# Rotary halves swapped by transfers inside SBUF instead of a matrix product, in a two-layer block kernel on one core

## What is computed

```python
def apply_rope(x, cos, sin):
    xf = x.astype(jnp.float32)
    x1, x2 = jnp.split(xf, 2, axis=-1)
    out = jnp.concatenate([x1 * cos - x2 * sin, x2 * cos + x1 * sin], axis=-1)
    return out.astype(x.dtype)
...
    u = jnp.einsum("bsd,de->bse", h, w_in)
    offs = np.cumsum(IN_SPLITS)[:-1].tolist()
    a_b, a_c, a_x, q, k, v, c_in = jnp.split(u, offs, axis=-1)

    y_a = a_b * causal_depthwise_conv(a_c * a_x, short_conv_w)

    q = apply_rope(q.reshape(b, s, 2, N_DIFF_HEADS, DIFF_HEAD_DIM), cos, sin)
    k = apply_rope(k.reshape(b, s, 2, N_DIFF_HEADS, DIFF_HEAD_DIM), cos, sin)
...
    o = diff_attention(q, k, v, lam)
...
    c = c_in + glu_b
    c = c[..., :CONF_WIDTH] * jax.nn.sigmoid(c[..., CONF_WIDTH:])
    c = causal_depthwise_conv(c, conf_dw_w) + conf_dw_b
    y_c = jax.nn.silu(layernorm(c, conf_ln_g, conf_ln_b))
```

## Time and profile before

| | us |
|---|---|
| median of 3 runs (lowest, highest) | 2680.19 (2677.57, 2681.05) |
| the profiled execution's own time | 2680.19 |
| its span in the trace | 2678.9 |
| PE busy | 2562.9 (96%) |
| DVE, ACT, POOL busy | 1103.3, 945.4, 1211.0 |

### The profile page before, as it was taken

One profiled execution on the slowest core, in us unless ns is written; L12 is line 12 of the kernel. 1 busy time (PEld: TensorE's weight loads), 2 busy tenths in 40 slices (PEclk: granted clock), 3 DMA queues, 4 the chain that ended last, 5 costly groups with the idle time before them and its releaser, 6 DMA issues.

```text
span 2678.9 us, 32969 instructions
## 1 busy us (share of the span) xinstructions
PE 2562.9 (96%) x12952; PEld 2112.5 (79%) x12952; DVE 1103.3 (41%) x2303; ACT 945.4 (35%) x1437; POOL 1211.0 (45%) x1597
## 2 busy tenths in 40 slices
PE   6999999999999999998999999999999999999998
PEld 5777888887777888886778788877777787888886
DVE  7965111126964211137656764423345523311112
ACT  4553322234453222244433233324453433322221
POOL 5114665653125656554332332344323554565653
PEclk8999999999999999999999999999998999999998
DMA  4442223225432222232110111122222231223222
GB/s 156 124 111 79 94 81 103 102 83 151 126 95 79 101 92 99 96 108 94 50 48 32 48 37 44 48 95 86 87 79 89 100 110 64 95 92 105 94 89 76
DMA packets 41371, 237.32 MB, mean 89 GB/s; under 512 B 4736, under 2 KB 5888, under 8 KB 18560
## 3 DMA queue, kind: packets, MB, share of 16 engines
q1 hardware_dynamic: 38912, 218.43, 23.4%
q0 software_dynamic: 2304, 16.78, 3.1%
HBM read 214.22 MB, written 4.19 MB: 82 GB/s over the span
## 4 chain that ended last, share of the span: by engine, by line
PE 84%; DVE 10%; ACT 3%; POOL 2%; issue 1%; DMA 0%; SPq 0%; DVEq 0%; ACTq 0%
PE PB L1757 67%; PE PB L1795 4%; PE PB L1759 4%; DVE cc L2413 2%; POOL WL L2788 2%; ACT WH L2016 1%; PE PB L1952 1%; PE PB L1971 1%; PE PB L1769 1%; PE PB L1777 1%; PE PB L1959 1%; PE PB L1919 1%; PE PB L1983 1%; PE PB L1999 1%; PE PB L1940 0%
## 5 line engine op out<-in xcount | busy, mean ns | idle before, releaser
L2788 POOL TENSOR_TENSOR WL<-WR,WH 128x256 fp32r<-128x256 f32 (+1 forms) x1444 | 1041.9, 757 | 789.1 <-ACT WH L2016 789.1
L1757 PE MATMUL PB<-HH,WH 128*128 128x512 f32 x1992 | 803.8, 404 | 12.2 <-ACT HH L2031 10.0
L1757 PE MATMUL PB<-HL,WH 128*128 128x512 f32 x1992 | 783.5, 393 | 1.9 <-DVE HL L2309 1.9
L1757 PE MATMUL PB<-HH,WL 128*128 128x512 f32 x1992 | 520.3, 397 | 2.6 <-POOL WL L2788 2.6
L2016 ACT ACTIVATE WH<-WR 128x2048 fp32r<-128x2048 f32 (+1 forms) x209 | 371.5, 1778 | 260.9 <-PE PB L1757 254.2
L1757 PEld LDWEIGHTS PB<-HH,WH 128*128 128x128 f32 x1992 | 378.4, 190 | 102.8 <-issue 14.3
L1757 PEld LDWEIGHTS PB<-HL,WH 128*128 128x128 f32 x1992 | 378.3, 190 | 80.0 <-issue 3.6
L1757 PEld LDWEIGHTS PB<-HH,WL 128*128 128x128 f32 x1992 | 366.0, 189 | 76.6 <-issue 3.9
L1757 PE MATMUL PB<-BL,WH 128*128 128x512 f32 x848 | 334.1, 394 | 0.8 <-DVE BL L2318 0.8
L1757 PE MATMUL PB<-BH,WH 128*128 128x512 f32 x784 | 310.6, 396 | 2.7 <-ACT BH L2045 2.7
L1757 PE MATMUL PB<-BH,WL 128*128 128x512 f32 x784 | 197.6, 396 | 5.4 <-POOL WL L2788 5.4
(11 more groups left out here) (344 smaller groups left out, 3103.1 us busy)
## 6 DMA issues: line engine op xcount, KB each, us to landing
WR<-in_w_gu SPq DMA_DIRECT2D x66, 1024.0 KB, 4.8
WR<-in_w_dn SPq DMA_DIRECT2D x48, 704.0 KB, 4.1
WR<-in_w_in SPq DMA_DIRECT2D x22, 1024.0 KB, 4.9
WL<-WR POOLq DMA_DIRECT2D x16, 1024.0 KB, 7.0
WR<-in_qkv SPq DMA_DIRECT2D x12, 1024.0 KB, 4.8
WR<-in_w_out SPq DMA_DIRECT2D x8, 1024.0 KB, 4.8
WR<-in_qk SPq DMA_DIRECT2D x8, 1024.0 KB, 4.8
WR<-in_gb SPq DMA_DIRECT2D x4, 1024.0 KB, 4.8
```

The costliest lines, as they stand in the source:

```text
L1757: ins = pe.matmul(out[:, 0:n], wt[:, k * cols + j * P:k * cols + (j + 1) * P], x[:, k, 0:n], start=first, stop=last)
L2788: ins = g.tensor_tensor(m.WL[u % 2][:, part], m.WR[u % 2][:, part], f32(m.WH[u % 2][:, part]), ALU.subtract)
```

## The change

The swap of halves is made by four transfers inside SBUF of 32 partitions each (64 KB), issued by SP, from qr into a new tile qs; the matrix product, its PSUM bank and its constant go. `qkin` becomes a plain copy out of PSUM on ACT (with the scale 0.125 for q). RSTD is multiplied once a layer into the cosine and sine tables (`scaled`, two DVE operations), which rotc and rots use. In the short convolution `sh1` multiplies by RSTD squared (made by ACT, `r2`) and `sh2` multiplies by the next PSUM tile directly. The planner's table gets costs on DVE for the gating (`glu`, 2.7) and `lam` (0.9), which had none, and a time of 4.0 from a swap's issue to its landing.

```diff
+    m.qs = at("qs0", [P, S], b0 + 10 * S * 4)[0], at("qs1", [P, S], b1 + 10 * S * 4)[0]
...
+    m.RCOS, m.RSIN, m.R2 = rcos, m.ct, rcos
...
-    "lnmul": [("V", 1.4, 0)], "lnact": [("A", 1.9, 0)], "qkin": [("V", 0.7, 0)], "vin": [("A", 0.5, 0)],
-    "rot": [("T", 0.9, 0), ("V", 1.5, 0)], "sh1": [("V", 0.9, 0)], "sh2": [("V", 1.5, 0)], "sh3": [("V", 2.2, 0)], "sh4": [("V", 1.5, 0)],
+    "glu": [("V", 2.7, 0)], "lam": [("V", 0.9, 0)], "lnmul": [("V", 1.4, 0)], "lnact": [("A", 1.9, 0)], "scaled": [("V", 1.4, 0)], "r2": [("A", 0.6, 0)], "qkin": [("A", 0.6, 0)], "vin": [("A", 0.5, 0)],
+    "rot": [("V", 1.5, 0)], "sh1": [("V", 0.9, 0)], "sh2": [("V", 0.8, 0)], "sh3": [("V", 2.2, 0)], "sh4": [("V", 1.5, 0)],
...
+SWAP_TIME = 4.0
...
+        if kind == "swap":
+            c.when[given["swapped"]] = t + SWAP_TIME
+            return {"end": t}
...
+        step("scaled", l, rope=rope, r=r, after=f + ct_after[0])
...
-        def rotate(name, c, q):
-            room = fbank.take()
-            t = Tile(room, room.after)
-            pe("rot", l, name, c, tile=t, q=q.i, tok=at("qkin", l, name, c), rope=rope, after=f)
-            room.free(at("rots", l, name, c))
-            q.free(at("rot", l, name, c))
+        def swap(name, c, q):
+            s = swaps.take()
+            swapped[s.i] += 16 * (P // 32)
+            done = f"swap{s.i}", swapped[s.i]
+            step("swap", l, name, c, q=q.i, s=s.i, tok=at("qkin", l, name, c), after=s.after + rope + f, swapped=done)
+            return name, c, q, s, done
+
+        def rotate(name, c, q, s, done):
+            step("rot", l, name, c, q=q.i, s=s.i, tok=at("qkin", l, name, c), after=f, swapped=done)
+            q.free(at("rots", l, name, c), at("rotc", l, name, c))
+            s.free(at("rot", l, name, c))
             turned[name, c] = True
...
-                    step("qkin", l, name, c, tile=t, q=q.i, r=r, after=q.after)
+                    step("qkin", l, name, c, tile=t, q=q.i, after=q.after)
                     room.free(at("qkin", l, name, c))
                     if waiting:
                         rotate(*waiting)
-                    waiting = (name, c, q)
+                    waiting = swap(name, c, q)
...
+            step("r2", l, r=r, after=[at("rotc", l, "k", 1), at("rotc", l, "k", 3)])
...
-        elif kind == "rot":
-            te.all(w["tile"].after)
-            te.wait_ge(*at("qkin", *key))
-            pe.matmul(PB[w["tile"].b][:], m.CON[:, C_SWAP:C_SWAP + P], m.qr[w["q"]][:], start=True, stop=True).then_inc(tile, 1)
...
+        elif kind == "qkin":
+            l, name, c = key
+            ae.wait_ge(*w["tile"].done)
+            ae.all(w["after"])
+            a.activation(m.qr[w["q"]][:], PB[w["tile"].b][:], ACT.Copy, scale=0.125 if name == "q" else 1.0).then_inc(sems["qkin"], 1)
+        elif kind == "r2":
+            ae.all(w["after"])
+            ae.wait_ge(*w["r"])
+            a.activation(m.R2[:], m.RSTD[:], ACT.Square).then_inc(sems["r2"], 1)
...
-        elif kind == "qkin":
-            l, name, c = key
-            ve.wait_ge(*w["tile"].done)
+        elif kind == "scaled":
+            l, = key
+            ve.all(w["rope"])
             ve.all(w["after"])
-            v.scalar_tensor_tensor(m.qr[w["q"]][:], PB[w["tile"].b][:], 0.125 if name == "q" else 1.0, m.RSTD[:],
-                                   ALU.mult, ALU.mult).then_inc(sems["qkin"], 1)
+            ve.wait_ge(*w["r"])
+            v.tensor_tensor(m.RCOS[:], m.COS[:], m.RSTD[:], ALU.mult).then_inc(sems["rcos"], 1)
+            v.tensor_tensor(m.RSIN[:], m.SIN[:], m.RSTD[:], ALU.mult).then_inc(sems["rsin"], 1)
         elif kind == "rot":
             l, name, c = key
-            q, dst = m.qr[w["q"]], (m.Q if name == "q" else m.K)
-            ve.wait_ge(*w["tile"].done)
-            ve.all(w["rope"])
+            turned, dst = m.qs[w["s"]], (m.Q if name == "q" else m.K)
+            ve.wait_ge(*w["swapped"])
+            ve.wait_ge(*at("rsin", l))
+            v.tensor_tensor(turned[:], turned[:], m.RSIN[:], ALU.mult).then_inc(sems["rots"], 1)
+            ve.wait_ge(*at("rots", *key))
             ve.wait_ge(*at("rotc", *key))
-            v.tensor_tensor(q[:], PB[w["tile"].b][:], m.SIN[:], ALU.mult).then_inc(sems["rots"], 1)
-            ve.wait_ge(*at("rots", *key))
-            v.tensor_tensor(dst[:, c, :], dst[:, c, :], q[:], ALU.add).then_inc(sems["rot"], 1)
+            v.tensor_tensor(dst[:, c, :], dst[:, c, :], turned[:], ALU.add).then_inc(sems["rot"], 1)
...
-            times_rstd(m.cx[:, 2:2 + S], w["tile"], "sh1")
+            ve.wait_ge(*w["tile"].done)
+            ve.wait_ge(*at("r2", l))
+            v.tensor_tensor(m.cx[:, 2:2 + S], PB[w["tile"].b][:], m.R2[:], ALU.mult).then_inc(sems["sh1"], 1)
         elif kind == "sh2":
             l, j = key
-            ve.all(w["after"])
-            times_rstd(m.ct[:], w["tile"], "sh2a")
-            ve.wait_ge(*at("sh2a", l, j))
-            v.tensor_tensor(m.cx[:, 2:2 + S], m.cx[:, 2:2 + S], m.ct[:], ALU.mult).then_inc(sems["sh2"], 1)
+            ve.wait_ge(*w["tile"].done)
+            ve.wait_ge(*at("sh1", l, j))
+            v.tensor_tensor(m.cx[:, 2:2 + S], m.cx[:, 2:2 + S], PB[w["tile"].b][:], ALU.mult).then_inc(sems["sh2"], 1)
...
-            ge.all(w["rope"])
+            ge.wait_ge(*at("rcos", l))
             ge.all(w["after"])
-            g.tensor_tensor(dst[:, c, :], m.qr[w["q"]][:], m.COS[:], ALU.mult).then_inc(sems["rotc"], 1)
+            g.tensor_tensor(dst[:, c, :], m.qr[w["q"]][:], m.RCOS[:], ALU.mult).then_inc(sems["rotc"], 1)
...
+        elif kind == "swap":
+            l, name, c = key
+            s = w["s"]
+            se.wait_ge(*at("qkin", *key))
+            se.all(w["after"])
+            for p in range(0, P, 32):
+                q.dma_start(m.qs[s][p:p + 32, :], m.qr[w["q"]][p ^ 32:(p ^ 32) + 32, :]).then_inc(sems[f"swap{s}"], 16)
```

More of the change, by code:

```diff
@@ L61 @@
 NVEC = _n
-C_ID, C_ONE, C_INVF, C_SGN, C_SWAP, C_CAUS, C_INCL, C_LEV, C_RST = 0, 128, 256, 257, 264, 392, 904, 1032, 1800
-NCON = 2312
+C_ID, C_ONE, C_INVF, C_SGN, C_CAUS, C_INCL, C_LEV, C_RST = 0, 128, 256, 257, 264, 776, 904, 1672
+NCON = 2184
 def constants():
@@ L232 @@
     "lnsum": (), "lnsub": ("V:lnsub",), "lnmul": ("V:lnmul",), "lnact": ("A:lnact",),
-    "qkin": ("V:qkin",), "rot": ("G:rotc", "V:rots", "V:rot"), "vin": ("A:vin",),
-    "sh1": ("V:sh1",), "sh2": ("V:sh2a", "V:sh2"), "sh3": ("V:sh3",), "sh4": ("V:sh4a", "V:sh4"),
+    "scaled": ("V:rcos", "V:rsin"), "r2": ("A:r2",), "qkin": ("A:qkin",), "swap": (), "rot": ("G:rotc", "V:rots", "V:rot"), "vin": ("A:vin",),
+    "sh1": ("V:sh1",), "sh2": ("V:sh2",), "sh3": ("V:sh3",), "sh4": ("V:sh4a", "V:sh4"),
     "score": (), "smax": ("V:smax0", "V:smax1"), "sexp": ("A:sexp",), "snorm": ("V:snorm",),
@@ L264 @@
     "rope_tab_v": "rt1 rt3 rt5", "rope_tab_a": "rt2 rt4", "lambda_v": "lam1 lam gg", "glu_v": "glu1 glu2 glu", "ln_v": "lnsub lnmul ssq2",
-    "rotate_v": "rots rot", "short_v": "sh1 sh2a sh2 sh3 sh4a sh4", "smax_v": "smax0 smax1", "squares_a": "ssq ssqa ssqb",
+    "rotate_v": "rcos rsin rots rot", "short_v": "sh1 sh2 sh3 sh4a sh4", "smax_v": "smax0 smax1", "squares_a": "ssq ssqa ssqb",
     "ffn_v": "ff1 ff3 ff", "gates_v": "rcol c1 ab dtb udt dcum rg rlast rlo", "gates_a": "beta edt alog ldt reg rdec rct rhi idr",
@@ L796, in ffn @@
         return toks, fo2
-    rope = []
+    rope, swapped = [], [0, 0]
     def block1(l, fo, then):
@@ L808, in block1 @@
         qrs = Ring([Room(0), Room(1)], clock)
-        for q in qrs.rooms:
+        swaps = Ring([Room(0), Room(1)], clock)
+        for q in qrs.rooms + swaps.rooms:
             q.free(*f)
@@ L903, in short_conv @@
             acc_after = [at("rot", l, "k", 1), at("rot", l, "k", 3)]
+            step("r2", l, r=r, after=[at("rotc", l, "k", 1), at("rotc", l, "k", 3)])
             for j in range(2):
                 room, t = yield from tiles_of(it)
-                step("sh1", l, j, tile=t, r=r, after=f)
+                step("sh1", l, j, tile=t, after=f)
                 room.free(at("sh1", l, j))
@@ L909, in short_conv @@
                 room, t = yield from tiles_of(it)
-                step("sh2", l, j, tile=t, after=ct_after[0])
-                room.free(at("sh2a", l, j))
+                step("sh2", l, j, tile=t)
+                room.free(at("sh2", l, j))
                 yield
@@ L915, in short_conv @@
                 room, t = yield from tiles_of(it)
-                step("sh4", l, j, tile=t)
+                step("sh4", l, j, tile=t, after=acc_after)
                 room.free(at("sh4a", l, j))
-                ct_after[0] = [at("sh4", l, j)]
                 step("opv", "mix", l, j, src=m.cacc[:], c=j, tok=at("sh4", l, j), after=b_after)
@@ L2462, in vector_program @@
             l, j = key
+            ve.all(w["after"])
             times_rstd(m.ct[:], w["tile"], "sh4a")
@@ L2831, in sync_program @@
```

(5 more changed lines are left out.)

6 lines of the change are left out of this document (2 added, 4 removed).

## The result

The changed kernel is slower by half a per cent: 2690.8 us median of 7 runs (2685.7 to 2701.2), before 2679.2 of 7 (2670.9 to 2682.0), ratio 1.0052 with an interval of 1.0031 to 1.0073. The profiled execution took 2694.8, its span is 2693.5.

A forecast was written before the change was run, and what follows sets the result against it. PE, busy 96% of the span, was taken as the bound. Of 29.0 us removed, 9.0 stayed in layer 0 and 1.0 in layer 1: 2680.2 - 10 = 2670 us; own range 2664 to 2677, outer range 2657 to 2684.

The forecast's parts named there:

- Layer 0, the swaps: Layer 0 rotations: swaps queue behind u5's load, q1's land at 67.5, and later waits return 4.3 us of the gain.
- serial pieces: Rival: swap pieces land one behind another, 13.6 us a pair against 8, 6 us lost in all, 2676; chance 0.07.
- the estimate of 8.6: Time in us of one swap if its four pieces go one after another, by the Trainium skill's fit.
- k0's copy on ACT: Layer 0: k0's copy waits until q0's rotation frees qr, at 68.9 against PE's need at 68.4, 0.5 us.
- The sum's 1.3 for the scores: Layer 0, on to the scores: 1.3 us more of the gain returned, leaving the kernel about 4 us ahead there.
- Layer 1: Layer 1 as a whole: 8.6 - 7.1 + 0.7 - 1.2, a gain of 1.0 us, bounds -6 and 6.
- layer 0's small waits: Layer 1: k0, k1 copies 0.5 and 2.4, v 1.4, low part 0.9, scores 1.9; 7.1 us returned.
- PE's first wait: Layer 0, head of the rotations: PE stops at 49.97 and starts again at 53.9, 3.9 us lost.
- The low part: Layer 0: POOL's split that the first k tile's low products and u5's load wait for, taken as done at 61.
- late swaps: Rival: swaps land late behind loads, DVE late at the scores, layer ends slower; 7 us lost, 2687; chance 0.11.
- Its point of decision: Late swaps decides from about 5.5 us between last piece's issue and landing, or if loads go no earlier than before.
- the 10.5 us wait: Layer 0: PE's one wait at the swap product for qkin on DVE, behind nine taps; 10.45 us counted as going.

The follow-up runs named there:

- e8: The changed kernel with all in-projection low parts subtracted by POOL, so no accumulating transfer runs beside the swaps; 2709.5 us, ratio 1.0123.
- e3: The kernel before with only the planner's two new DVE costs (glu 2.7, lam 0.9); 2666.6 us, ratio 0.9958.
- e6: The kernel before with the new prices, scaled tables and qkin copy on ACT; swap on PE and short convolution as before; 2677.4 us, ratio 0.9995.
- e9: e2 with the planner told that qkin costs DVE 0.7 though it runs on ACT; 2671.7 us, ratio 0.9986.
- e2: The changed kernel with the swap as a product on PE again, the rest as changed; 2675.2 us, ratio 0.9997.
- e5: The kernel before with the new prices and the changed short convolution; qkin on DVE, swap on PE; 2659.7 us, ratio 0.9930.
- e1: The changed kernel with each pair of swaps ahead of the weight load it stood behind in SP's list; 2666.5 us, ratio 0.9955.

## Why the prediction was wrong

**The failed step** is "Layer 0, the swaps": "I take 4 from the last issue, 67.5". It was 71.9: the landing took 8.7 us, not 4. The first piece was issued at 61.24, as forecast; q0's four pieces were to be issued by 63.5 and to land within 4 us, inside bounds of 1.7 and 5.9 from single rows. I priced a transfer beside one 1 MB load. POOL's accumulating transfer, for which I had the row and used it only in the rival, starts at 61.83 in the same place, and e8 shows that it is 4.6 of the 10.7 us from first issue to landing. Of the 16 swaps, which were all to land within 6.5 us of their first issue, 8 took longer, up to 11.8. Undisturbed, a piece lands in 2.0 and the four overlap: 3.9 us from the first issue to the last landing. That rules out the rival "serial pieces", and the estimate of 8.6 for four pieces one after another, which came from a fit for transfers that GpSimd issues. The view of the transfers issued in 79 to 81 us:

```profile
qs<-qr SPq DMA_DIRECT2D x4, 64.0 KB, 2.0
```

**What hangs on it.** k0's copy on ACT was to cost PE 0.5, 2.4 and 1.4 us; PE waited 5.07 and 0.98. The forecast had no clock loss there. The window behind the wait has one:

```profile
68.25:73.32 5.07, 0.00 (x1) 0.00 (x0) 1.39 (x3) 0.60 (x1) 0.00 (x0) 0.86 0.77 176
73.32:79.00 5.68, 5.50 (x25) 5.21 (x25) 5.65 (x8) 0.66 (x2) 1.77 (x1) 0.52 0.62 220
```

In 5.68 us at 0.52 half the time is lost, 2.7. DVE's list then runs nearly as I had added it up (21.1 us from the first rotation to the maxima, 19.1 forecast; one tap took 2.20), but from 71.9: 92.96 instead of 86.6. DVE was idle for 13.22 us with a full list behind; I had taken 9 and called them free until the scores, where PE then waited 2.5. The sum's 1.3 for the scores had no row of its own: by the same sum DVE was 4.5 us ahead there.

**Layer 1** was mis-sized for the same reason, and more: -1.0 forecast, +9.6 measured. q0's swap took 11.8 us there, beside an accumulating transfer issued in the same instant (656.94). Carrying over layer 0's small waits (7.1 in all) missed that k0's copy costs PE 6.2 there, with a lower clock behind it (0.70 granted in 670 to 680 us), and that the head norms would wait 3.4; and there was no long wait whose end could pay for it.

**What was right.** PE's first wait: 3.9 forecast, 3.82. The low part: 61 forecast, 60.70, with the half clock ahead of it. u5's load right behind its low part. The rival "late swaps" was the mechanism, with its place: DVE late behind a swap that stands behind a load. Its point of decision, 5.5 us from the last piece's issue to its landing, was passed: 8.7, from 63.1 to 71.9. That its 2687 is near the 2690.8 measured is partly luck: it had the load at 62.24 (60.72 measured), the pieces in 5.9 and the maxima at 90.2 (92.96), and it priced the accumulating transfer only for what that itself loses. Its chance of 0.11 was too small, because DVE's lack of room, which I had listed as the case for it, holds in every row of that stage that I had read.

**The second omission** is one of attribution. I costed the prices at nothing of their own and gave the end of the 10.5 us wait to qkin's move to ACT. e3 shows that the prices alone cut it to 2.8, and e6 that tables and copy on ACT cost what the prices gave. Why they cost that stays open. e9's marker speaks for the planner, which lays 30 taps ahead of the first maxima in e2 and 27 in e9 (PE waits 3.3 us there in e2 and 2.0 in e9). e5 has nearly e9's order (28 taps) with qkin on DVE; their markers are 2.7 us apart, but their ratios, 0.9930 and 0.9986, differ clearly. A trial of the very same order with either engine was not made.

**In sum**, by the markers: prices -14.0, tables with the copy on ACT and the convolution +11.3 (e3 to e2), transfers +15.5 (e2 to the changed kernel), together +12.8; transfers placed ahead of the loads are -7.0 instead of +15.5. The timed ratios give the same steps as about -11, +10 (at the edge of the intervals), +15 and -11. The best version found leaves out both the transfers and the tables with the copy on ACT: prices and convolution, 0.9930.

## What to carry to other kernels

A transfer that replaces a short operation has the price of its place in the queue and of what flies beside it, not its own: list every transfer that starts in the same microseconds, those of other queues too, before taking a landing time. Where a queue is in order, put the small urgent transfer ahead of the large load that waits for something late; it held two loads up by 2.3 and 4.5 us here and was still worth 24 us. And when a change edits a planner's costs along with the work, time the costs alone first: filler work ahead of a first consumer is a wait that looks like the consumer's.

## What the hardware showed that I had not expected

Issuing is not free of what is in flight. The issue of a 64 KB piece took 0.59 us as a rule and up to 1.90 (the source view above), so that the eight issues of q0 and q1 took 8.90 us of SP's time instead of the 5.02 of e1. The weight load is hardly the cause: in e8 the eight issues right behind the same load took 5.0 us too (one later piece took 1.31). In layer 1 of e1, with the accumulating transfer and no weight load in flight, the eight took 8.7.

Behind the marker PE has the same 7446 records in the same order in all kernels, and yet this part took between 1425.6 and 1442.4 us in their profiled executions. Two of them:

```profile
1231.08:2671.50 1440.42, 1372.70 (x7446) 1145.01 (x7446) 582.28 (x1292) 500.96 (x852) 625.46 (x833) 0.97 0.22 75
```

```profile
1229.80:2655.40 1425.60, 1358.46 (x7446) 1133.36 (x7446) 582.43 (x1292) 501.11 (x852) 628.62 (x833) 0.99 0.22 76
```

The first is e3 (from 0.07 us ahead of its marker on), the second e9. PE was busy 14.2 us longer in the slower one, at a granted clock of 0.97 against 0.99: the stretches at half clock fell differently. Timed runs of one kernel go with the clock too: before took 2667.8 at a mean granted clock of 0.987 and 2689.3 at 0.977. The 17 us of this part are as much as most of these experiments' differences, which is why the marker ahead of it stands beside each total. Whether the marker scatters less from execution to execution is not shown, since each kernel has one profile.
